# Gate tables of a sparse expert layer: one 256-column product a token instead of a full-precision one, with the row gathers spread over other slots

## The chip, the cores and the metric

One Trainium2 chip, one core. The metric is the device time of one launch in microseconds (us), lower is better. A time is the median of several runs; a profiled execution is one run taken with the hardware profiler.

## The reference

One transformer block in f32 for 256 tokens of width 2048: an input projection, two mixers (a gated linear attention and a compressed, selected and windowed attention), a gated merge, an output projection with residual, and then the part that matters here, a product-key expert layer over 128 x 128 = 16384 experts with 8 heads and 16 picks a head:

```python
v1, i1 = lax.top_k(s1, PEER_TOPK)
v2, i2 = lax.top_k(s2, PEER_TOPK)
cand = (v1[..., :, None] + v2[..., None, :]).reshape(T, PEER_HEADS, PEER_TOPK * PEER_TOPK)
vals, flat = lax.top_k(cand, PEER_TOPK)
e1 = jnp.take_along_axis(i1, flat // PEER_TOPK, axis=-1)
e2 = jnp.take_along_axis(i2, flat % PEER_TOPK, axis=-1)
experts = e1 * PEER_NKEYS + e2
gates = jax.nn.softmax(vals, axis=-1)
...
hid = jax.nn.gelu(jnp.einsum('cd,chkd->chk', xc, u_tab[ec]).astype(jnp.float32))
return jnp.einsum('chk,chkd->cd', (gc * hid).astype(xc.dtype), v_tab[ec])
```

Each token has 128 picks, each a pair (e1, e2) with a gate. The block ends in a norm.

## The kernel before, in words

The kernel doesn't gather the picked experts of most tokens. It streams all 16384 rows of both expert matrices past TensorE in 128 weight units each (1 MB, 128 x 2048) and multiplies the hidden values by a table of gates, 128 x 128 a token, that is zero where nothing was picked. The first 32 tokens (G) are done otherwise: their rows of both matrices are gathered by index, 64 gathers of 128 rows, one row product on VectorE each (`gathered`, L1782). The first half of the gathers are rows of the first matrix.

**Units.** Every weight unit is loaded by SyncE (L339), split into an upper part by ScalarE (`hi_wide`, L577, a copy to the short f32 form) and a lower part by VectorE (`lo_wide`, L1396, weight minus upper part), and used by TensorE in 16 chunks with two products each, 448 and 224 columns (L1265, L1266 in the first pass, L1314, L1315 in the second). Four buffers hold split units; the split of a unit may start when the unit four before it is done (`unit_done`), so ScalarE and VectorE work three units ahead (AHEAD).

**Rounds.** The first pass is 16 rounds i of 8 units k, `hidden(i)` on each engine: TensorE L1249, ScalarE L850, VectorE L1816, GpSimd L503 to L524. After each second unit ScalarE copies the sums out of PSUM (L868), GpSimd adds their two halves (`hidden_sum`, L467), ScalarE applies Gelu (L844) and stores every fourth unit's worth to HBM. In rounds 0 to 7 VectorE also does the routing of 16 groups (`route`, L1721) and GpSimd its lookups (`lookup`, L472). PSUM banks 0 to 3 take the units, banks 4 to 7 are free for tables.

**The table stage** is rounds 8 to 14: two tables of 16 tokens (TB) a round, 14 in all. For each, VectorE writes in `picks_hot` (L1743) a one-hot of e1 for 16 tokens at once (L1754) and, token by token, a one-hot of e2 times the gate (L1758). TensorE multiplies the two for each token, 128 x 128, after units 2 and 6 (`table`, L1285, L1292); both operands are full f32, which the trace shows as two passes a token. ScalarE copies the 16 tables out of PSUM into `gate_a`, rearranged so that the 16 tokens lie side by side (`table_out`, L817, L825), and stores them. `turn_picks` and `picks_out` turn the picks of 128 tokens at a time before that.

**What sets the order** is written by hand: each engine runs its own list in order, with semaphores between them. Row products stand in the slots PRE_SLOTS (L91) of the first pass (32 of them, PRE) and V_SLOTS (L94) of the second (32); GpSimd issues their loads by PRE_ISSUE and one after each hidden_sum from round 8 on. In the second pass VectorE has, in each pair of units, two splits and `weights` (L1806): a product with the gate tables and a subtraction, with a ScalarE copy between.

The lines of VectorE's `hidden` that order the work in a unit:

```python
if k % 4 == 0 and tables:
    tb = i * 2 + (k // 4 - 2 * I_TAB)
...
    picks_hot(tb)
lo_wide(i * 8 + (U0 + k + AHEAD), k + AHEAD)
...
if isinstance(i, int) and (i, k) in pre_slots:
    gathered(pre_slots[i, k])
```

## Time and profile before

| what | us |
|---|---|
| median of 3 runs (2312.88 to 2314.02) | 2313.14 |
| the profiled execution | 2312.33 |
| its span, first to last instruction | 2310.6 |
| TensorE busy in the span | 2277.3 |
| VectorE, ScalarE, GpSimd busy | 1665.7, 1215.1, 472.9 |
| VectorE's 256 lower splits at L1402 | 587.4 |
| ScalarE's 14 table copies at L825 | 54.1 |
| mean granted TensorE clock, as a share of full speed | 0.997 |

The profiled execution is timed as the others are; the rest of it beside the span, 1.7 us, lies before the first and after the last instruction. "Idle before" in a row is the time in which the engine stood still before the instruction, with what released it. A row of a timeline gives start, duration, engine, line, operation and operands. Starts that follow each other more closely than the duration mean that the instructions overlap, as the long rows of products on TensorE and of splits on VectorE do.

### The profile page before, as it was taken

What the parts mean: (1) busy time and instruction counts of PE and PEld (TensorE: products, weight loads), DVE (VectorE), ACT (ScalarE), POOL (GpSimd) and SP (SyncE); (2) the same over time, 40 slices, a digit from 0 to 9 for tenths busy, and PEclk for the clock granted to TensorE, in tenths of its full rate; (3) what the DMA queues carried; (4) which work ended last, traced back from release to release, by engine and by line L of the source; (5) the groups of instructions that cost most, each with busy time, mean ns of one, the idle gap of its engine ahead of it and who ended that gap; (6) DMA issues with size and microseconds to landing.
All of it is one profiled execution on the core that took longest, in us unless ns stands there. A gap on an engine that the chain in (4) does not pass through costs nothing.

```text
span 2310.6 us, 35967 instructions
## 1 busy us (share of the span) xinstructions
PE 2277.3 (99%) x13406; PEld 2074.6 (90%) x13406; DVE 1665.7 (72%) x2049; ACT 1215.1 (53%) x1138; POOL 472.9 (20%) x430
## 2 busy tenths in 40 slices
PE   7999999999999999999999999999999999999997
PEld 6888888888888889999999999999999999999997
DVE  5544776665655555898899989887578778878775
ACT  5534555555454344666666556565544444444443
POOL 0001342100000000243456322222222222122100
PEclk9999999999999999999999999999999999999999
DMA  7756556545456656666676899999999999999982
GB/s 283 271 193 214 209 202 213 196 164 172 169 200 219 223 198 237 224 240 237 227 279 246 318 328 333 331 329 316 353 365 360 362 361 366 364 373 368 355 314 87
DMA packets 122285, 623.73 MB, mean 270 GB/s; under 512 B 12000, under 2 KB 40928, under 8 KB 61776
## 3 DMA queue, kind: packets, MB, share of 16 engines
q1 hardware_dynamic: 58752, 423.65, 49.6%
q0 software_dynamic: 25616, 156.65, 18.2%
q10 hardware_dynamic: 37824, 42.18, 5.1%
q8 instruction: 60, 0.98, 0.2%
q14 instruction: 33, 0.27, 0.0%
HBM read 576.29 MB, written 46.14 MB: 269 GB/s over the span
## 4 chain that ended last, share of the span: by engine, by line
PE 92%; DVE 4%; ACT 2%; DMA 1%; issue 1%; DVEq 0%; POOL 0%; ACTq 0%; SPq 0%; POOLq 0%
PE psum L1314 18%; PE psum L1265 17%; PE psum L957 10%; PE psum L959 10%; PE psum L958 10%; PE psum L1266 9%; PE psum L1315 8%; PE psum L1292 2%; DVE w_lo L1402 1%; PE psum L1091 1%; DMA w_raw<-in_w_units 1%; PE psum L1216 1%; PE psum L1215 1%; PE psum L1217 1%; PE psum L1052 1%
## 5 line engine op out<-in xcount | busy, mean ns | idle before, releaser
L1265 PE MATMUL psum<-h2T,w_hi 128*128 128x448 f32 x2048 | 644.6, 373 | 1.1 <-DVE w_lo L1402 0.7
L1314 PE MATMUL psum<-w_ul,w_hi 128*128 128x448 f32 x2048 | 642.7, 374 | 1.8 <-DVE w_ul L1812 1.8
L1266 PE MATMUL psum<-h2T,w_lo 128*128 128x224 f32 x2048 | 543.3, 265 | 0.0
L1315 PE MATMUL psum<-w_ul,w_lo 128*128 128x224 f32 x2048 | 541.2, 264 | 0.0
L1394 DVE TENSOR_TENSOR w_lo<-w_raw,w_hi 128x2048 fp32r<-128x2048 f32 x144 | 331.3, 2306 | 213.6 <-ACT w_hi L575 213.1
L1314 PEld LDWEIGHTS psum<-w_ul,w_hi 128*128 128x128 f32 x2048 | 384.1, 188 | 31.7 <-issue 2.6
L1265 PEld LDWEIGHTS psum<-h2T,w_hi 128*128 128x128 f32 x2048 | 383.8, 187 | 31.2 <-issue 1.2
L575 ACT ACTIVATE w_hi<-w_raw 128x2048 fp32r<-128x2048 f32 x144 | 275.5, 1913 | 253.3 <-DMA w_raw<-in_w_units 225.2
L1315 PEld LDWEIGHTS psum<-w_ul,w_lo 128*128 128x128 f32 x2048 | 390.7, 191 | 0.0
L1266 PEld LDWEIGHTS psum<-h2T,w_lo 128*128 128x128 f32 x2048 | 390.2, 191 | 0.0
L1402 DVE TENSOR_TENSOR w_lo<-raw_x,w_hi 128x2048 fp32r<-128x2048 f32 x128 | 294.2, 2301 | 76.8 <-ACT w_hi L587 74.7
L1402 DVE TENSOR_TENSOR w_lo<-w_raw,w_hi 128x2048 fp32r<-128x2048 f32 x128 | 293.2, 2292 | 68.2 <-ACT w_hi L587 65.6
L957 PE MATMUL psum<-w_hi,hT_hi 128*128 128x512 f32 x768 | 306.2, 399 | 12.0 <-DVE w_lo L1394 12.0
L959 PE MATMUL psum<-w_hi,hT_lo 128*128 128x512 f32 x768 | 300.5, 391 | 0.0
L958 PE MATMUL psum<-w_lo,hT_hi 128*128 128x512 f32 x768 | 300.1, 391 | 0.0
L587 ACT ACTIVATE w_hi<-w_raw 128x2048 fp32r<-128x2048 f32 x128 | 244.8, 1913 | 99.0 <-PE psum L1315 51.9
L587 ACT ACTIVATE w_hi<-raw_x 128x2048 fp32r<-128x2048 f32 x128 | 244.0, 1908 | 58.0 <-PE psum L1315 37.3
L470 POOL TENSOR_TENSOR hs<-hs 128x448 f32<-128x448 f32 x64 | 105.2, 1643 | 422.9 <-ACT hs L868 416.9
L879 ACT ACTIVATE w_ul<-h_in 128x896 fp32r<-128x896 f32 x64 | 61.0, 954 | 244.3 <-DVE h_in L1809 244.3
L957 PEld LDWEIGHTS psum<-w_hi,hT_hi 128*128 128x128 f32 x768 | 145.0, 189 | 41.2 <-issue 12.9
L959 PEld LDWEIGHTS psum<-w_hi,hT_lo 128*128 128x128 f32 x768 | 144.7, 188 | 31.1
L958 PEld LDWEIGHTS psum<-w_lo,hT_hi 128*128 128x128 f32 x768 | 145.0, 189 | 28.7
(331 smaller groups left out, 2807.3 us busy)
## 6 DMA issues: line engine op xcount, KB each, us to landing
w_raw<-in_w_units SPq DMA_DIRECT2D x272, 1024.0 KB, 5.8
raw_x<-in_w_units SPq DMA_DIRECT2D x128, 1024.0 KB, 6.3
g_tab<-tab_scratch POOLq DMA_DIRECT2D x32, 896.0 KB, 8.0
h_in<-hid_scratch POOLq DMA_DIRECT2D x64, 448.0 KB
hid_scratch<-hst ACTq DMA_DIRECT2D x32, 448.0 KB, 5.1
tab_scratch<-gate_a ACTq DMA_DIRECT2D x14, 1024.0 KB, 7.0
proj_scratch<-evac ACTq DMA_DIRECT2D x24, 512.0 KB, 5.2
x_nat<-in_x POOLq DMA_DIRECT2D x2, 2048.0 KB, 9.2
```

What stands on the lines that cost most here:

```text
L470: pool.tensor_tensor(both, both, hs[:, q, :, NU:2 * NU], ALU.add).then_inc(hid_summed, 1)
L575: act.activation(w_hi[:, s % SPLIT, :], w_raw[:, s % RAW, :], ACT.Copy).then_inc(hi_done, 1)
L587: act.activation(w_hi[:, s % SPLIT, :], src, ACT.Copy).then_inc(hi_done, 1)
L957: pe.matmul(out, xh[:, kc0 + c, ts], rh, start=st, stop=False, skip_group_check=True)
L958: pe.matmul(out, xh[:, kc0 + c, ts], rl, start=False, stop=False, skip_group_check=True)
L959: ins = pe.matmul(out, xl[:, kc0 + c, ts], rh, start=False, stop=en, skip_group_check=True)
L1265: pe.matmul(psum[:, k % 4, 0:2 * NU].rearrange("p (a t) -> p a t", a=2), uh, h2T[:, c, :, G:S], start=c == 0, stop=False, skip_group_check ...
L1266: ins = pe.matmul(psum[:, k % 4, NU:2 * NU], ul, h2T[:, c, 0, G:S], start=False, stop=c == KC - 1, skip_group_check=True)
L1314: pe.matmul(psum[:, c, 0:2 * NU].rearrange("p (a t) -> p a t", a=2), w_hi[:, s, o:o + P], ul, start=first, stop=False, skip_group_check=True)
L1315: return pe.matmul(psum[:, c, 0:NU], w_lo[:, s, o:o + P], ul[:, 0, :], start=False, stop=False, skip_group_check=True)
L1394: dve.tensor_tensor(w_lo[:, s % SPLIT, :], w_raw[:, s % RAW, :], w_hi[:, s % SPLIT, :].bitcast(F32), ALU.subtract).then_inc(lo_done, 1)
L1402: dve.tensor_tensor(w_lo[:, s % SPLIT, :], src, w_hi[:, s % SPLIT, :].bitcast(F32), ALU.subtract).then_inc(lo_done, 1)
```

## The change

Each operand of the table product becomes a short f32 one (F32R): the one-hot of e1 as it is, and the one-hot of e2 times the gate's upper part and times its lower part, side by side in 256 columns. So a token has one product of 256 columns, and the two halves of its result are added afterwards. This is done for 8 tokens (TH) at a time, after units 1, 3, 5 and 7 of rounds 8 to 14, 28 half-tables (NHALF). VectorE writes both one-hots of 8 tokens in one instruction (`picks`), ScalarE scales the second by the upper gate, token by token (`table_slot`), GpSimd by the lower gate (`second_lower`). After the product ScalarE copies the lower results out of PSUM (`lower_out`), ahead of its weight copy in the even units, and VectorE adds them to the upper results, into the rearranged buffer (`table_added`). The store goes out after every second half-table. The rows: 25 in the first pass, 7 of them before round 8 (5 before), 39 in the second pass.

```diff
-PRE = 32
-PRE_EARLY = 5
+TH = TB // 2
+NHALF = 2 * NTAB
+PRE = 25
+PRE_EARLY = 7
...
-PRE_SLOTS = [(5, 3), (5, 7), (6, 3), (6, 7), (7, 3)] + [(I_TAB + (2 * n + 5) // 8, (2 * n + 5) % 8) for n in range(PRE - PRE_EARLY)]
-PRE_ISSUE = {(4, 3): 0, (5, 2): 1, (6, 0): 2, (6, 2): 3, (7, 0): 4}
+PRE_ROUND = {8: (3, 7), 9: (1, 3, 5), 10: (1, 5), 11: (1, 3, 5), 12: (1, 5), 13: (1, 3, 5), 14: (1, 5), 15: (1,)}
+PRE_SLOTS = [(4, 7), (5, 3), (5, 7), (6, 3), (6, 7), (7, 3), (7, 7)] + [(i, k) for i in PRE_ROUND for k in PRE_ROUND[i]]
+PRE_ISSUE = {(4, 2): 0, (5, 0): 1, (5, 2): 2, (6, 0): 3, (6, 2): 4, (7, 0): 5, (7, 2): 6}
...
-V_SLOTS = sorted([(0, 5)] + [(i, k) for i in range(1, U_IT - 1) for k in (1, 5)] + [(2, 7), (6, 7), (10, 7)])
+V_SLOTS = sorted([(0, 5), (0, 7)] + [(i, k) for i in range(1, U_IT - 1) for k in (1, 5)] + [(i, 3) for i in range(2, 11)])
...
+        tables = psum[:, 4:8, :].rearrange("p b (t s c) -> p (b t) s c", s=2, c=PEER_NK)
+        staged = gate_a[:, :, :].rearrange("p a b -> p (a b)").rearrange("p (c t) -> p t c", t=TB)
...
+            def second_lower(hb):
+
+                pool.wait_ge(picks_done, hb + 1)
+                if hb:
+                    pool.wait_ge(tab_done, hb)
+                pool.tensor_tensor(hot2a[:, :, 1, :], picked[:, 1, :, :].bitcast(F32),
+                                   gate_lo[:, G + hb * TH:G + (hb + 1) * TH, None].to_broadcast([P, TH, PEER_NK]), ALU.mult).then_inc(hot2_done, 1)
...
             for i in range(I_TAB, I_END):
                 for j in range(4):
+                    second_lower((i - I_TAB) * 4 + j)
                     hidden_sum(i * 4 + j, j % 2)
...
+            def lower_out(i, k):
+                hb = 4 * (i - I_TAB) + k // 2
+                if 1 <= hb <= NHALF:
+                    act.wait_ge(tab_done, hb)
+                    if hb == 1:
+                        act.wait_ge(lookup_done, ROUTES)
+                    else:
+                        act.wait_ge(tab_out, hb - 1)
+                    act.activation(low[:, :, :], tables[:, :, 1, :], ACT.Copy).then_inc(low_out, 1)
+
+            def table_slot(i, k):
+                hb = 4 * (i - I_TAB) + k // 2
+                if k % 2 == 0:
+                    if hb < NHALF:
+                        act.wait_ge(picks_done, hb + 1)
+                        if hb:
+                            act.wait_ge(tab_done, hb)
+                        for j in range(TH):
+                            t = G + hb * TH + j
+                            ins = act.activation(hot2a[:, j, 0, :], picked[:, 1, j, :].bitcast(F32), ACT.Copy, scale=gate_hi[:, t:t + 1].bitcast(F32))
+                        ins.then_inc(hot2_done, 1)
+                elif k % 4 == 1 and 0 < hb <= NHALF:
+                    tb = hb // 2 - 1
+                    act.wait_ge(tab_out, hb)
+                    act.dma_start(tab[:, :, tb, :].rearrange("g p n -> p g n"),
+                                  gate_a[:, :, :].rearrange("p a b -> p (a b)").rearrange("p (g n) -> p g n", g=U_IT)).then_inc(tab_st, 16)
...
                 for k in range(8):
+                    if tables and k % 2 == 0:
+                        lower_out(i, k)
                     hi_wide(i * 8 + (U0 + k + AHEAD), k + AHEAD)
...
-                    if k % 4 == 3 and tables:
-                        table_out(i * 2 + (k // 4 - 2 * I_TAB))
+                    if tables:
+                        table_slot(i, k)
...
-                    if k % 4 == 2 and tables:
-                        table(i * 2 + (k // 4 - 2 * I_TAB))
+                    if k % 2 == 1 and tables:
+                        table(i * 4 + (k // 2 - 4 * I_TAB))
...
+                pe.wait_ge(picks_done, hb + 1)
+                pe.wait_ge(hot2_done, hb * 2 + 2)
+                if not (isinstance(hb, int) and hb == 0):
+                    pe.wait_ge(tab_out, hb)
+                for j in range(TH):
+                    ins = pe.matmul(tables[:, j, :, :], picked[:, 0, j, :], hot2a[:, j, :, :], start=True, stop=True, skip_group_check=True)
                 ins.then_inc(tab_done, 1)
...
+            def picks(hb):
+
+                if hb:
+                    dve.wait_ge(hot2_done, 2 * hb)
+                    dve.wait_ge(tab_done, hb)
+                dve.tensor_tensor(picked[:, :, :, :], iota[:, None, None, :].to_broadcast([P, 2, TH, PEER_NK]),
+                                  rtT[:, 0:2, G + hb * TH:G + (hb + 1) * TH, None].to_broadcast([P, 2, TH, PEER_NK]), ALU.is_equal).then_inc(picks_done, 1)
+
+            def table_added(hb):
+
+                dve.wait_ge(low_out, hb + 1)
+                if hb == 0:
+                    dve.wait_ge(hg_done, 1)
+                elif hb % 2 == 0:
+                    dve.wait_ge(tab_st, 16 * (hb // 2))
+                dve.tensor_tensor(staged[:, hb % 2 * TH:(hb % 2 + 1) * TH, :], tables[:, :, 0, :], low[:, :, :], ALU.add).then_inc(tab_out, 1)
...
+                    hb = 4 * (i - I_TAB) + k // 2
+                    if k % 2 == 0 and tables and 1 <= hb <= NHALF:
+                        table_added(hb - 1)
+                    if k % 2 == 0 and tables and hb < NHALF:
+                        if G + hb * TH in (G, P):
+                            gates_split((G + hb * TH) // P)
+                        picks(hb)
                     lo_wide(i * 8 + (U0 + k + AHEAD), k + AHEAD)
```

Left out here: buffers and semaphores that are renamed or moved; `gates_split`, which cuts the gates of 128 tokens into their upper and lower parts on VectorE in two small instructions, twice in all; the loads of keys and iota, which now share one semaphore; the gathers' issue rounds on GpSimd (two slots of rows ahead); the row indices, made one unit earlier, in (4, 1); and the Gelu of the gathered rows on ScalarE, which moves from (0, 1) to (2, 7) of the second pass.

## Rows read from the trace of the kernel before

**Rows 1.** The page's first part: busy us (share of the span) x instructions

```profile
PE 2277.3 (99%) x13406; PEld 2074.6 (90%) x13406; DVE 1665.7 (72%) x2049; ACT 1215.1 (53%) x1138; POOL 472.9 (20%) x430
```

**Rows 2.** The chain of waits in the table stage: start us, us, what

```profile
1286.21 5.44 PE psum L1292 x32
1406.52 3.58 PE psum L1292 x32
1430.15 3.58 PE psum L1292 x32
```

**Rows 3.** TensorE's wait (us, times, longest); window: us, PE PEld DVE ACT POOL busy, PEclk, DMA, GB/s

```profile
PE psum L1292 <- DVE hot2a L1758: 1.9, 1, 1.9
1284.00:1292.00 8.00, 6.13 (x38) 5.87 (x37) 7.96 (x14) 2.69 (x3) 2.77 (x1) 0.79 0.36 112
```

**Rows 4.** VectorE in order of time in the table stage: start us, us

```profile
1413.16 2.29 DVE L1754 TENSOR_TENSOR hot1a<-iota,rt 128x2048 f32<-128x2048 f32 x1
1415.37 5.04 DVE L1758 TENSOR_SCALAR hot2a<-iota,rt 128x128 f32<-128x128 f32 x16
```

**Rows 5.** ScalarE's groups by line, mean ns before the last bar

```profile
L825 ACT ACTIVATE gate_a<-psum 128x2048 f32<-128x2048 f32 x14 | 54.1, 3865 | 27.7 <-PE psum L1292 27.7
L587 ACT ACTIVATE w_hi<-raw_x 128x2048 fp32r<-128x2048 f32 x128 | 244.0, 1908 | 58.0 <-PE psum L1315 37.3 <-PE psum L1266 19.3 <-PE psum L1217 1.0
L738 ACT ACTIVATE sm<-sm,nmx 128x128 f32<-128x128 f32 x32 | 12.4, 387 | 0.0
```

**Rows 6.** TensorE in order of time: 256 columns, then the end of a unit

```profile
899.73 0.28 PE L1217 MATMUL psum<-h2T,w_hi 128*128 128x256 f32 x1
899.85 0.28 PE L1215 MATMUL psum<-h2T,w_hi 128*128 128x256 f32 x1
1406.26 0.26 PE L1266 MATMUL psum<-h2T,w_lo 128*128 128x224 f32 x1
1406.36 3.74 PE L1292 MATMUL psum<-hot2a,hot1a 128*128 128x128 f32 x32
```

**Rows 7.** VectorE and GpSimd in order of time in the routing stage

```profile
1252.26 0.69 DVE L1740 TENSOR_TENSOR hot<-abf,iota 128x512 f32<-128x512 f32 x1
1252.87 2.29 DVE L1402 TENSOR_TENSOR w_lo<-raw_x,w_hi 128x2048 fp32r<-128x2048 f32 x1
1253.10 3.21 POOL L474 TENSOR_TENSOR hot<-hot,if_top 128x512 f32<-128x512 f32 x1 [1.20 <-DVE hot L1740]
1255.07 3.38 DVE L1798 CUSTOM_DVE_ANT_0 pre_ring<-pre_ring,g 128x2048 f32<-128x2048 f32 x1
```

**Rows 8.** GpSimd by line: ns min/median/max, first and last start us

```profile
L474 POOL TENSOR_TENSOR hot<-hot,if_top x16: 1284/1301/3350, 970.0 to 1275.2; 128x512 f32<-128x512 f32 x16
L499 POOL TENSOR_TENSOR g<-g,x_rep x1: 4660/4660/4660, 957.7 to 957.7; 128x2048 f32<-128x2048 f32 x1
L470 POOL TENSOR_TENSOR hs<-hs x64: 1147/1294/3302, 962.3 to 1645.3; 128x448 f32<-128x448 f32 x64
```

**Rows 9.** VectorE by line: ns min/median/max

```profile
L1659 DVE TENSOR_TENSOR x_nat<-x_nat,psum x4: 1221/1222/1222, 824.2 to 892.1; 128x1024 f32<-128x1024 f32 x4
L1493 DVE TENSOR_TENSOR blk_c<-kvT_c,posT x4: 1868/1882/1900, 120.9 to 126.2; 128x960 f32<-128x960 f32 x4
```

**Rows 10.** The stores of gate_a: from issue to landing

```profile
DMA to landing us min/median/max: 5.9/7.0/19.5
```

**Rows 11.** VectorE and GpSimd in order of time before the first table

```profile
1277.39 3.15 DVE L1754 TENSOR_TENSOR hot1a<-iota,rt 128x2048 f32<-128x2048 f32 x1
1282.43 0.32 POOL L479 TENSOR_TENSOR rt<-hot 128x32 f32<-128x32 f32 x1
```

**Rows 12.** VectorE in order of time in the routing stage

```profile
1162.45 2.29 DVE L1402 TENSOR_TENSOR w_lo<-w_raw,w_hi 128x2048 fp32r<-128x2048 f32 x1 [1.13 <-ACT w_hi L587]
```

**Rows 13.** Windows of the second expert pass, columns as in group 3

```profile
1725.30:1765.40 40.10, 40.10 (x258) 38.27 (x257) 31.06 (x19) 18.73 (x12) 8.04 (x9) 1.00 0.91 357
1765.40:1805.50 40.10, 40.10 (x258) 38.28 (x257) 33.17 (x20) 18.72 (x12) 10.88 (x10) 1.00 0.96 372
```

More of the change, by code:

```diff
@@ L456, in _ @@
             pool.wait_ge(xt_done, 4)
-            pool.dma_start(keys[:, :, :], io["keys"]).then_inc(keys_in, 16)
-            pool.dma_start(iota[:, :], io["iota"].partition_broadcast(P)).then_inc(iota_in, 16)
+            pool.dma_start(keys[:, :, :], io["keys"]).then_inc(keys_iota_in, 16)
+            pool.dma_start(iota[:, :], io["iota"].partition_broadcast(P)).then_inc(keys_iota_in, 16)
             def v_load(m):
@@ L858, in hidden @@
                         route_exp(i * 2 - 1)
-                    if tile is not None and k == 2 * tile:
+                    if tile is not None and k == tile:
                         picks_out(tile)
-                    if k % 4 == 3 and tables:
-                        table_out(i * 2 + (k // 4 - 2 * I_TAB))
+                    if tables:
+                        table_slot(i, k)
                     if k % 2 == 1:
@@ L886, in _ @@
                 hidden(i, routes=True)
-            hidden(I_TAB, tables=True)
-            hidden(I_PICK1, tile=1, tables=True)
-            with act.Fori(I_PICK1 + 1, I_END) as i:
-                hidden(i, tables=True)
-            hidden(I_END)
+            for i in range(I_TAB, I_END + 1):
+                hidden(i, tile=1 if i == I_PICK1 else None, tables=True)
             hidden_out(U_IT - 1, 3)
@@ L916, in gathered_gelu @@
                 act.activation(hid_g[:, :], dots[:, :], ACT.Gelu_apprx_tanh, scale=rs_g[:, 0:1]).then_inc(hidg_done, 1)
-            experts_out(0, gelu=1)
-            with act.Fori(1, U_IT // 2 - 1) as i:
+            for i in range(2):
+                experts_out(i)
+            experts_out(2, gelu=7)
+            with act.Fori(3, U_IT // 2 - 1) as i:
                 experts_out(i)
@@ L1283, in turn_picks, with table @@
                 ins.then_inc(rt_turned, 1)
-            def table(tb):
-                pe.wait_ge(hot1_done, tb + 1)
-                pe.wait_ge(hot2_done, tb + 1)
-                if not (isinstance(tb, int) and tb == 0):
-                    pe.wait_ge(tab_out, tb)
-                for j in range(TB):
-                    ins = pe.matmul(psum[:, 4 + j // 4, (j % 4) * P:(j % 4 + 1) * P], hot1a[:, j, :], hot2a[:, j, :], start=True, stop=True, skip_group_check=True)
+            def table(hb):
+                pe.wait_ge(picks_done, hb + 1)
[4 more added lines that the diff above has]
+                    ins = pe.matmul(tables[:, j, :, :], picked[:, 0, j, :], hot2a[:, j, :, :], start=True, stop=True, skip_group_check=True)
                 ins.then_inc(tab_done, 1)
@@ L1741, in route, with gates_split @@
                                       iota[:, None, None, 0:TOPK].to_broadcast([P, 2, TOPK, TOPK]), ALU.is_equal).then_inc(lookup_in, 1)
-            def picks_hot(tb, parts=range(5)):
-                hot1, hot2 = hot1a, hot2a
-                for part in parts:
-                    if part == 0:
-                        if not (isinstance(tb, int) and tb == 0):
-                            dve.wait_ge(hot2_done, tb)
-                            dve.wait_ge(tab_done, tb)
-                        dve.tensor_copy(rt16[:, :, :], rtT[:, :, ds(tb * TB + G, TB)]).then_inc(rt16_done, 1)
-                        dve.wait_ge(rt16_done, tb + 1)
-                        dve.tensor_tensor(hot1[:, :, :], iota[:, None, :].to_broadcast([P, TB, PEER_NK]),
-                                          rt16[:, 0, :, None].to_broadcast([P, TB, PEER_NK]), ALU.is_equal).then_inc(hot1_done, 1)
-                    else:
-                        for j in range((part - 1) * TB // 4, part * TB // 4):
-                            ins = dve.tensor_scalar(hot2[:, j, :], iota[:, :], rt16[:, 1, j:j + 1], rt16[:, 2, j:j + 1], ALU.is_equal, ALU.mult)
-                        if part == 4:
-                            ins.then_inc(hot2_done, 1)
+            def gates_split(t):
+                dve.wait_ge(rt_out, t + 1)
+                cols = slice(t * P, (t + 1) * P)
+                step(dve.tensor_copy(gate_hi[:, cols], rtT[:, 2, cols]))
+                dve.tensor_tensor(gate_lo[:, cols], rtT[:, 2, cols], gate_hi[:, cols].bitcast(F32), ALU.subtract)
+            def picks(hb):
[11 more added lines that the diff above has]
+                dve.tensor_tensor(staged[:, hb % 2 * TH:(hb % 2 + 1) * TH, :], tables[:, :, 0, :], low[:, :, :], ALU.add).then_inc(tab_out, 1)
             def gather_rows():
@@ L1833, in hidden @@
                         clear_pads()
-                    if isinstance(i, int) and (i, k) in pre_slots:
+                    if (i, k) in pre_slots:
                         gathered(pre_slots[i, k])
@@ L1847, in _ @@
                 hidden(i, routes=True)
-            for i in range(I_TAB, I_END):
+            for i in range(I_TAB, I_END + 1):
                 hidden(i, tables=True)
-            hidden(I_END)
             def experts_out(i, last=False):
```

73 lines of the change are left out of this document (31 added, 42 removed).

## The prediction, made before the changed kernel ran

> **What bounds the kernel now.** The page first: TensorE is busy 2277.3 of 2310.6 us [rows 1]. Then the chain of waits through the table stage (the last 7 of 16 rounds of the first expert pass): it runs on TensorE's products and its tables, and a table of 16 tokens starts each 23.63 us, 3.58 of it the table, the rest four weight units, so 5.01 a unit [rows 2]. TensorE waits there for nothing but, once, the first table [rows 3]. So TensorE time saved is time saved, as long as the other engines' chain from one table to the next stays under TensorE's.
>
> **What is removed.** 13 tables at 3.58 = 46.5 us. The first cost more: its waiting of 1.9 us, then 5.44, with the granted clock at 0.79 in the 8 us around it, that is partly at the lower of the two levels (1.2 GHz) after TensorE had idled [rows 2, 3]; together 7.3. Sum 53.8. VectorE loses the first one-hot and the 16 scaled ones of every 16 tokens (2.3 + 5.0) [rows 4], ScalarE its 3.86 us copy [rows 5]. Fourteen of these go.
>
> **What is added on TensorE.** 28 half-tables of 8 products, each 256 columns. Such products start 0.12 us apart in the query stage [rows 6]: 0.96, with the restart 1.04, and 29.1 in all. Bounds: nothing less than 0.10 (the 224-column product's step [rows 6]), at most the 0.22 that a token takes now, 3.58 for 16. With every new wait hidden that is 53.8 - 29.1 = 24.7 us gained.
>
> **The chain that replaces it.** The buffer of one-hots is single, PSUM is single (8 tokens x 256 columns fill banks 4 to 7), so table h+1 can't be prepared beside table h: product, ScalarE's copy of the lower half, VectorE's table_added, VectorE's picks, then ScalarE's 8 scaled copies and GpSimd's second_lower side by side, then the next product. Count from x, the end of one picks on VectorE:
> - VectorE's weight split is queued directly behind: to x+2.2 (start to start 2.21 [rows 4]).
> - GpSimd gets its signal at x but both read two SBUF operands. In the routing stage the same sequence stands: VectorE's one-hot ends at 1252.95, its split starts, GpSimd's multiply, released by that one-hot, takes 3.21 instead of 1.30, ending 1.15 after the split, and the row product behind, with as many elements as the split's 2.29, takes 3.38 [rows 7, 8]. They exclude each other, and the one that waits gets the next turn. The Trainium skill agrees (GPSIMD Engine Reference, "Key points": the SBUF interfaces are shared, with contention where VectorE has two SBUF inputs).
> - second_lower has 1024 elements: between half of 4.66 and 1.30 plus its share of the rest, 2.3 to 2.4 [rows 8]. It runs from x+2.2 to x+4.6; there the next table may start.
> - ScalarE: 8 scaled copies of 128. The nearest row takes 0.39 each, with overlap and accumulation [rows 5]; on the slope from its larger copies 0.2. I take 0.24: 1.9, then its weight copy 1.8: x+3.8. VectorE's second split waits for the multiply: x+4.6 to x+6.8.
> - GpSimd's hidden_sum (1.1 at its shortest [rows 8]) has its turn next, to x+7.9; if this round has a row, 2.2 more, to x+10.1.
> - table_added: a. picks: 2.2. The next x is at x + 12.3 + a.
>
> **The value of a.** It adds 1024 elements from PSUM and SBUF and writes them 64 bytes apart. Lower end 1.22, the same shape written densely [rows 9]. But ScalarE's present copy writes this very pattern and takes 3.86 for 2048, where a dense one takes 1.91 [rows 5], and VectorE reading 960 elements 64 bytes apart takes 1.88 [rows 9]. Both are 1.8 to 1.9 ns an element, so a = 2.0, the nearest rows in layout. Two pages of the Trainium skill differ here: VectorE: DVE Perf Modes ("Mode 1×") says of that mode that weird strides and PSUM operands "all work" at one result a cycle, which would give the lower end; SBUF — State Buffer ("Door 1: The DMA port swizzle", the note on cachelines) says that each access in a new 16-byte line pays a penalty. The trace's reads bear out the second; no run here shows the write on VectorE.
>
> **Rounds.** A round with a row therefore takes 14.3 us. One without: TensorE sets it, 10.02 + 1.04 = 11.06, since the chain (0.96 product, 1.1 copy, 2.0, 2.2, 4.6 = 10.9) just fits. In rounds of even number a second wait enters: VectorE's next table_added overwrites what ScalarE stores, and the store is issued after the second weight copy, at x+3.8, and lands 5.9 to 7.0 later [rows 10]: next x = x+3.8+5.9+2.0+2.2 = 13.9 to 15.0. With fewer rows on the queues I take the lower part, level with 14.3. Of 27 rounds 17 have a row between (the slots of round 8 to (14,5)), one even round has none: 18 x 14.3 + 9 x 11.1 = 357.3.
>
> **The first table.** Due after 2 units instead of 3. VectorE reached its one-hots at 1277.4, 8 us late; the row added at (7,7) moves that by 3.1, splitting the gates by 0.6, so picks end near 1283.5, the last lookup on GpSimd ends at 1282.75 [rows 11], and second_lower at about 1288: TensorE waits 8.9 us.
>
> **The sum over the stage.** Before: 12 units (60.2) + 7.3 + 13 x 23.63 = 374.6. After: 10 units (50.1) + 8.9 + 357.3 + 1.0 = 417.4. That is +42.8. Behind the new waits stand, on ScalarE, the weight copies (three units ahead of need), and on GpSimd hidden_sum and the row loads, each ahead of its user by a round: nothing beyond the turns counted. SyncE's weight loads wait for the second splits and follow TensorE at its new pace: nothing. picks_out, the Gelu of the rows, and the wait for keys and iota together move into idle time: nothing; if they did not, under 1 us each. Before the stage, one row more at (4,7): VectorE idles only 1.13 us for ScalarE afterwards [rows 12] and is behind at the end, so of 2.3 to 3.4 us some 2.0 reach TensorE (0 to 3.4). In the second pass 7 rows more: a stretch with a third row has VectorE at 33.2 of 40.1 us instead of 31.1, DMA at 0.96 instead of 0.91, TensorE full in both [rows 13]; 0.5 (0 to 3). Sum +45.3 on the profiled execution's 2312.33, which is 0.8 under the median of the runs: 2358.
>
> **The rivals.** *Cheap add* (a = 1.22): a row round's chain is 13.5, of which an isolated one hides 0.9 in the slack of the round before: about 13.1, 18 x 1.2 less: 2336. For: the dense rows; against: both strided rows. The rule of the Trainium skill's VectorE: DVE Perf Modes ("Mode 1×") is this case. *Stores late or clock low*: landing at 7.0 or more adds 0.8 in 13 even rounds, and waits of 3 us may let the clock fall as at the first table, each such table then 1 us longer where it is on the chain (9): 2368. For: the median landing, the 0.79. *The cover holds* (the other side): GpSimd's multiply and sum run beside VectorE's splits and rows. Then 3.5 us of the row round's chain are gone; the point at which it decides is 11.06, which needs a near 1.2 and landing near 5.9 as well. Stage: 50.1 + 8.9 + 27 x 11.06 + 1.0 = 358.6, -16.0, with 2.5 of rows elsewhere 2299; with the remaining row slips up to 2308. Against: [rows 7]. For: stores and lookups move where the traffic is thinner, and records of GpSimd are rough. That the products are slower than 0.12 would sit inside the waits of the slow rounds; at the upper bound the nine fast ones grow by 0.8, 7 us.
>
> **How the numbers follow.** Chances: forecast 0.38, cheap add 0.24, late stores or clock 0.15, cover holds 0.18, something between that ends level 0.05. Range 2302 to 2374: from inside the case in which the cover holds to the late case with some microseconds more; outside stay most of the first and the tail of the last. A measurement of this kernel tells about 0.2% (4.6 us) from no change. Faster 0.18, same 0.05, slower 0.77.
>
> **What would show it.** Right: TensorE waits for GpSimd's second_lower before most tables, some 3 us where a row lies between, none or little where none does; second_lower near 4.3 us against 2.4 of work; VectorE's strided add near 2.0; store to landing 6 to 7 with VectorE waiting for it in some even rounds; the first table near 9 us late. Wrong: no waits for second_lower and tables 11.06 apart (cover holds), table_added at 1.2, or TensorE waits in the second pass.

## The result, and the profile after

The changed kernel takes 2354.7 us (median of 4 runs, 2352.55 to 2357.04), the kernel before 2313.0 beside it: a ratio of 1.0182, 95% interval 1.0169 to 1.0194. It is 1.8% slower; 2358 was forecast. The profiled execution took 2352.55, its span is 2350.9, 40.3 more than before.

The first part of its page answers to [rows 1]:

```profile
PE 2273.0 (97%) x13182; PEld 2063.6 (88%) x13182; DVE 1689.0 (72%) x1857; ACT 1249.4 (53%) x1376; POOL 624.8 (27%) x458
```

TensorE is busy 4 us less in a span 40 longer, and GpSimd has 152 us more. By the starts of the weight units on TensorE the 40.3 split up so: the part from the first unit to unit (8,0) takes 327.6 instead of 325.4 (+2.2), the table stage, from (8,0) to the first unit of the second pass, 411.6 instead of 376.0 (+35.6), the second pass to the end 668.7 instead of 666.6 (+2.2); the start of the first unit differs by 0.2.

What TensorE waits for in the table stage (us, times, longest), where [rows 3] had 1.9 us once:

```profile
PE psum L1332 <- POOL hot2a L503: 32.9, 12, 9.0
PE psum L1332 <- issue: 7.0, 4, 2.6
```

L1332 are the table's products, L503 is second_lower. The longest wait, 9.0, is the first table. From there the tables start 11.1 to 15.4 apart, where the kernel before kept its 23.63 for two halves [rows 2]. Here is one round with a row, in order of time, first VectorE, then ScalarE and GpSimd (start us, us):

```profile
1451.52 2.27 DVE L1795 TENSOR_TENSOR picked<-iota,rtT 128x2048 fp32r<-128x2048 f32 x1
1453.71 2.27 DVE L1442 TENSOR_TENSOR w_lo<-w_raw,w_hi 128x2048 fp32r<-128x2048 f32 x1
1458.12 2.29 DVE L1442 TENSOR_TENSOR w_lo<-raw_x,w_hi 128x2048 fp32r<-128x2048 f32 x1 [2.14 <-ACT w_hi L613]
1460.33 3.25 DVE L1842 CUSTOM_DVE_ANT_0 pre_ring<-pre_ring,g 128x2048 f32<-128x2048 f32 x1
...
1463.51 1.94 DVE L1805 TENSOR_TENSOR gate_a<-psum,low 128x1024 f32<-128x1024 f32 x1
1465.30 2.27 DVE L1795 TENSOR_TENSOR picked<-iota,rtT 128x2048 fp32r<-128x2048 f32 x1
...
1453.83 2.46 ACT L862 ACTIVATE hot2a<-picked,gate_hi 128x128 fp32r<-128x128 f32 x8 [2.54 <-DVE picked L1795]
1456.19 1.90 ACT L613 ACTIVATE w_hi<-raw_x 128x2048 fp32r<-128x2048 f32 x1
...
1453.87 3.87 POOL L503 TENSOR_TENSOR hot2a<-picked,gate_lo 128x1024 fp32r<-128x1024 f32 x1 [3.10 <-DVE picked L1795]
1459.03 2.40 POOL L487 TENSOR_TENSOR hs<-hs 128x448 f32<-128x448 f32 x1 [1.29 <-ACT hs L909]
```

Read it from x, the end of the picks, at 1453.79. VectorE splits to x+2.2, then waits 2.14 us; its second split starts at x+4.33, the row at 6.54, the add at 9.72, the next picks at 11.5, and the next x is 13.78 later. Ten of the 17 rounds with a row take this long (13.70 to 13.78), six take longer and wait for the store, and one takes 12.86. VectorE's wait is for ScalarE's weight copy (ends at x+4.30), which stands behind the eight scaled copies (2.46 together). second_lower ends at x+3.95, with 3.87 for a work that took 1.89 the one time that VectorE left it alone (the first), and the row takes 3.25 instead of 2.28 because hidden_sum has a turn in it. TensorE's product can start at x+4.0, so TensorE waits for GpSimd, but the loop that sets the pace runs through VectorE's own list and its 2.14 us wait for ScalarE's weight copy.

VectorE's own waits in the stage, the ones for w_lo before the first table included (us, times, longest):

```profile
DVE w_lo L1442 <- ACT w_hi L613: 74.7, 36, 6.0
DVE gate_a L1805 <- DMA tab_scratch<-gate_a: 8.1, 6, 2.1
DVE gate_a L1805 <- ACT low L851: 4.1, 5, 1.9
```

27 rounds take 351.4 from the first x to the last: 17 with a row between, 233.9 at 13.76 and 5.9 more, mostly the store's; and 10 without, 111.6 (10.65 where nothing disturbs). The granted clock falls in eight stretches of the stage, one beside the 9.0 us wait and seven beside waits of TensorE of 1.9 to 4.2 us; one wait of 2.5 us, at 1589.5, is left without. Two windows, columns as in [rows 3]:

```profile
1420.00:1430.00 10.00, 9.25 (x60) 8.57 (x58) 8.56 (x6) 3.83 (x6) 2.26 (x2) 1.00 0.64 253
1430.00:1440.00 10.00, 7.03 (x31) 6.70 (x32) 7.14 (x6) 7.34 (x10) 6.27 (x3) 0.66 0.61 212
```

0.66 over 10 us is some 7 at 1.2 GHz and the rest at 2.4. TensorE had waited 3.7 us for the table at 1432.97; its eight products then took 2.08 instead of the usual 1.21. In the windows of 10 us from 1280 to 1660 this adds up to 44 us at the lower level. It costs little, since most of it eats waiting that would be there anyway: what it delays on the loop is the lower copy, and VectorE waited for that 4.1 us in all, whatever the clock's part in it.

### The profile page after: what moved, and what is told of

It reads as the page before. It is cut to its first block, busy times and chain, and to the rows that moved or that the text cites. A ratio compares the mean times of both kernels' runs of the same rounds, so it can differ in the third digit from the quotient of the medians.

```text
span 2350.9 us, 35582 instructions
## 1 busy us (share of the span) xinstructions
PE 2273.0 (97%) x13182; PEld 2063.6 (88%) x13182; DVE 1689.0 (72%) x1857; ACT 1249.4 (53%) x1376; POOL 624.8 (27%) x458
## 4 chain that ended last, share of the span: by engine, by line
PE 77%; DVE 10%; ACT 5%; issue 4%; DMA 3%; POOL 1%; ACTq 0%; DVEq 0%; SPq 0%; POOLq 0%
PE psum L1354 17%; PE psum L997 10%; PE psum L999 10%; PE psum L1305 10%; PE psum L998 10%; PE psum L1355 8%; PE psum L1306 5%; DVE w_lo L1442 3%; DVE picked L1795 3%; ACT w_hi L613 2%; DMA tab_scratch<-gate_a 2%; ACT hot2a L862 2%; PE psum L1131 1%; POOL hot2a L503 1%; DVE gate_a L1805 1%
## 5 line engine op out<-in xcount | busy, mean ns | idle before, releaser
L1305 PE MATMUL psum<-h2T,w_hi 128*128 128x448 f32 x2048 | 656.3, 378 | 2.0 <-DVE w_lo L1442 2.0
L1305 PEld LDWEIGHTS psum<-h2T,w_hi 128*128 128x128 f32 x2048 | 390.5, 191 | 33.7 <-issue 3.0
L1306 PEld LDWEIGHTS psum<-h2T,w_lo 128*128 128x128 f32 x2048 | 396.6, 194 | 0.0
L997 PE MATMUL psum<-w_hi,hT_hi 128*128 128x512 f32 x768 | 305.9, 398 | 13.3 <-DVE w_lo L1434 13.3
L997 PEld LDWEIGHTS psum<-w_hi,hT_hi 128*128 128x128 f32 x768 | 144.7, 188 | 42.8 <-issue 14.6
L487 POOL TENSOR_TENSOR hs<-hs 128x448 f32<-128x448 f32 x64 | 123.1, 1923 | 219.3 <-ACT hs L909 193.9
```

Source lines behind the costliest of these rows:

```text
L487: pool.tensor_tensor(both, both, hs[:, q, :, NU:2 * NU], ALU.add).then_inc(hid_summed, 1)
L997: pe.matmul(out, xh[:, kc0 + c, ts], rh, start=st, stop=False, skip_group_check=True)
L1305: pe.matmul(psum[:, k % 4, 0:2 * NU].rearrange("p (a t) -> p a t", a=2), uh, h2T[:, c, :, G:S], start=c == 0, stop=False, skip_group_check ...
L1306: ins = pe.matmul(psum[:, k % 4, NU:2 * NU], ul, h2T[:, c, 0, G:S], start=False, stop=c == KC - 1, skip_group_check=True)
```

## The experiments

**Which of two links holds the second split.** The forecast's step was GpSimd's turn, the trace says ScalarE's copy. Three kernels, one edit each and both together; the first edit leaves out seven eighths of the lower multiply:

```diff
-                pool.tensor_tensor(hot2a[:, :, 1, :], picked[:, 1, :, :].bitcast(F32),
-                                   gate_lo[..., None].to_broadcast([P, TH, PEER_NK]), ALU.mult).then_inc(hot2_done, 1)
+                n = 1 if hb else TH
+                pool.tensor_tensor(hot2a[:, 0:n, 1, :], picked[:, 1, 0:n, :].bitcast(F32),
+                                   gate_lo[..., None].to_broadcast([P, n, PEER_NK]), ALU.mult).then_inc(hot2_done, 1)
```

> From the changed kernel (2354.7 us); GpSimd's second_lower multiplies the full 8 tokens for the first half-table only, and 1 token of 8 from then on (the lower part of the gates of the other 7 is left out of the tables). Forecast's step (GpSimd's turn on the operand interfaces is what the second weight split waits for): the second split starts at x+2.2 to x+3.9 instead of behind the multiply, and each row round loses about 2: 17 x 2 = 34 us, 2321. Rival A, from the trace of after: the second split starts 4.33 after the picks end because ScalarE's weight copy, queued behind the eight scaled copies, ends at 4.29, and the multiply ends at 3.95; then the split stays at 4.33, row rounds stay at 13.76, only the product comes some 1.5 us sooner and waits on ScalarE's copies: within 4 us of the changed kernel, 2351 to 2356.

```diff
-                    hi_wide(i * 8 + (U0 + k + AHEAD), k + AHEAD)
+                    if not (tables and k % 2 == 1):
+                        hi_wide(i * 8 + (U0 + k + AHEAD), k + AHEAD)
+                    if tables and k % 2 == 0:
+                        hi_wide(i * 8 + (U0 + k + 1 + AHEAD), k + 1 + AHEAD)
```

> From the changed kernel; ScalarE makes the weight copy of the odd unit ahead of the eight scaled copies instead of behind them. Nothing is left out. ScalarE idles up to 6.5 us before the picks, so the copy is finished by x and costs the scaled copies nothing. Rival A of the first run: the second split no longer waits for ScalarE, but then GpSimd's multiply, which has its turn from 2.2 to 3.95, is what it waits for: it starts at 3.95 instead of 4.33, so a row round takes 13.4: 17 x 0.38 = 6.5 us less, 2348. If ScalarE alone held it (no exclusion), the split would start at 2.2 and a row round would take 11.7: 2318. Forecast's step: 4.6 for the multiply's end stays, so no gain: 2354.

> Both edits together: 1 token of 8 in GpSimd's multiply, and the odd unit's weight copy ahead of the scaled copies. If the two links (ScalarE's copy, GpSimd's turn) stand side by side, each hiding the other, then only both together pay: the second split starts at 2.2 to 2.5, a row round takes 13.76 - 2.1 = 11.7, the others are set by TensorE at 11.06: 17 x 2.1 = 36 us less, 2319, and the waits of TensorE nearly go. If the sum of the two single runs is all (6.5 us), some third thing (the row, the store, the copy of the lower half) sets the round.

Measured, in that order: 2353.7 (2348.1 to 2356.4), 2349.2 (2343.9 to 2355.3) and 2333.8 (2331.4 to 2336.5). In the first, a row round still takes 13.77, and TensorE waits no less than before, now for ScalarE's scaled copies (31.7 us, 12 times, beside 9.1 for the first table): taking GpSimd's work away alone gave nothing. (Even with one token of 8 its record is 2.38 long, since it waits for its turn behind the first split.) The second split in the three kernels, in that order, from the rows in order of time (start us, us), with GpSimd's multiply behind it in the second:

```profile
1458.97 2.29 DVE L1443 TENSOR_TENSOR w_lo<-raw_x,w_hi 128x2048 fp32r<-128x2048 f32 x1 [2.13 <-ACT w_hi L614]
```

```profile
1453.74 4.00 DVE L1445 TENSOR_TENSOR w_lo<-raw_x,w_hi 128x2048 fp32r<-128x2048 f32 x1
...
1451.71 3.87 POOL L503 TENSOR_TENSOR hot2a<-picked,gate_lo 128x1024 fp32r<-128x1024 f32 x1 [6.24 <-DVE picked L1798]
```

```profile
1463.64 2.50 DVE L1446 TENSOR_TENSOR w_lo<-w_raw,w_hi 128x2048 fp32r<-128x2048 f32 x1
```

With the copy first, the split is issued at once but takes 4.00: it stands still while GpSimd's multiply has its turn after the first split, and ends 0.5 earlier than in the changed kernel. A row round takes 13.27; in the medians the 5 us are within the spread of the runs. With both links gone it takes 2.50 and most row rounds come to 10.9 to 11.6. So the two links stand side by side, each hiding the other, as expected for the third run. But it came out 15 us above the 2319 expected, most of it in the next wait:

```profile
DVE gate_a L1809 <- DMA tab_scratch<-gate_a: 31.0, 5, 8.8
```

Five rounds of this kernel, of 15.4 to 21.2 us, are those in which the add waits for the store. The faster loop uncovers it.

**The row and the store.** The rows' VectorE work cut to a sixteenth, and the store cut to a sixteenth (both leave the rest of that work out):

```diff
+                if PRE_EARLY <= n < PRE:
+                    row = row[:, 0:128]
+                    ins = dve.tensor_tensor_reduce(row, row, hg[:, 0:128], 1.0, 0.0, ALU.mult, ALU.add, dots[:, j:j + 1])
+                    ins.then_inc(ring_used, 1)
```

> From the changed kernel; the 18 rows numbered 7 to 24 are still loaded, but VectorE multiplies 128 of their 2048 elements (the dot products of these rows are left out). It prices the row in the round. Forecast: a row costs 14.3 - 11.1 = 3.2 in each of 17 rounds, 54 us of the stage, 2300. From the trace of after: VectorE's row of 3.24 goes, the chain of a round is 10.6 and TensorE sets 11.06, so 17 x 2.7 = 46 us less, less what the store's landing keeps in even rounds (up to 5 us): 2309 to 2314. Rival: the store of the even rounds sets the pace without the rows too (13.9 in 13 rounds): 2335 or more.

```diff
-                    act.dma_start(tab[:, :, tb, :].rearrange("g p n -> p g n"), gate_a[...]).then_inc(tab_st, 16)
+                    act.dma_start(tab[0:1, :, tb, :].rearrange("g p n -> p g n"), gate_a[...][:, 0:1, :]).then_inc(tab_st, 16)
...
-                pool.dma_start(g_tabs[i % 2][:, :, :], tab[i % U_IT]).then_inc(vt_in[i % 2], 16)
+                pool.dma_start(g_tabs[i % 2][:, :, :], tab[0]).then_inc(vt_in[i % 2], 16)
```

> From the changed kernel: each store of a finished table writes group 0 of its 16 groups only, and the second pass reads group 0 each time (so 15 of 16 parts of each table are left out, the transfers of the second pass stay in size). It prices the wait for the store and its traffic. The trace of after shows 8.1 us of VectorE's waiting for it in 6 even rounds; in row rounds all of it is on the path: 8 us less, 2346.5, the even rounds all at 13.76. Forecast's step (store issued at x+3.8, landing 5.9 to 7.0, even rounds 13.9 to 15.0, level with the row's 14.3) gives at most 1 to 2 us: 2353. Rival: thinner traffic also speeds the row loads and weight loads: nothing waits for these, so no more than 8.

Short rows: 2342.4 (2334.0 to 2344.5), 12 us less where 41 to 46 had been expected. Two things took the place of the row. Its short form still takes 1.25 where hidden_sum has its turn, so such a round takes 11.8, not 10.6; and the add waited 24.9 us for stores instead of 8.1. The row in order of time, and VectorE's wait:

```profile
1470.57 1.25 DVE L1843 CUSTOM_DVE_ANT_0 pre_ring<-pre_ring,g 128x128 f32<-128x128 f32 x1
```

```profile
DVE gate_a L1805 <- DMA tab_scratch<-gate_a: 24.9, 6, 5.9
```

Short store: 2346.2 (2343.1 to 2347.3), the 8 us as expected, and 13 of the 17 row rounds at 13.76 or 13.77, the other four shorter. The store is worth 8 us as the kernel stands, and more as soon as the loop gets shorter.

**The add.** Its elements walked in the other order, and written densely (which leaves out their placing in the table):

```diff
-                dve.tensor_tensor(staged[...], tables[:, :, 0, :], low[:, :, :], ALU.add).then_inc(tab_out, 1)
+                dve.tensor_tensor(staged[...].rearrange("p t c -> p c t"), tables[:, :, 0, :].rearrange("p t c -> p c t"),
+                                  low[:, :, :].rearrange("p t c -> p c t"), ALU.add).then_inc(tab_out, 1)
```

> From the changed kernel, nothing left out: table_added walks its 1024 elements column by column with the 8 tokens innermost (reads of PSUM and low far apart, writes in runs of 32 bytes) instead of token by token (reads dense, writes 64 bytes apart, 1.95 us). If the spacing of the writes alone makes the 1.95 (the forecast's reason for a = 2.0), it falls to near the dense 1.22 and 17 row rounds give 12 us: 2342. If spacing on the reading side costs as much (one operand or two), it stays at 1.9 or rises to 2.5 or more, and the round with it: 2354 to 2370.

```diff
-                dve.tensor_tensor(staged[:, hb % 2 * TH:(hb % 2 + 1) * TH, :], tables[:, :, 0, :], low[:, :, :], ALU.add).then_inc(tab_out, 1)
+                dve.tensor_tensor(gate_a[:, hb % 2 * TH:(hb % 2 + 1) * TH, :], tables[:, :, 0, :], low[:, :, :], ALU.add).then_inc(tab_out, 1)
```

> From the changed kernel; table_added writes its half-table densely instead of 64 bytes apart (the placing of the entries in the table is left out, the store sends the same bytes). It prices the spacing of the writes. If the spacing is what takes 1.95, the add falls to about 1.22 (the dense row of the kernel before) and 17 row rounds give 0.73 each: 12 us, 2342. If it is the read from PSUM or the pairing of PSUM with SBUF, it stays near 1.95 and nothing changes: 2354.

The add by line (ns min/median/max), in the changed kernel, in the other order, and dense:

```profile
L1805 DVE TENSOR_TENSOR gate_a<-psum,low x28: 1871/1952/2010, 1294.1 to 1643.5; 128x1024 f32<-128x1024 f32 x28
```

```profile
L1805 DVE TENSOR_TENSOR gate_a<-psum,low x28: 1981/2013/2076, 1295.2 to 1643.2; 128x1024 f32<-128x1024 f32 x28
```

```profile
L1805 DVE TENSOR_TENSOR gate_a<-psum,low x28: 1212/1219/1226, 1294.2 to 1645.4; 128x1024 f32<-128x1024 f32 x28
```

The write's spacing is the whole difference: dense it is 1.22, the lower bound of the forecast. The other order, with dense runs of 32 bytes on the writing side and the spacing on the reading side, is no better (2354.8, 2353.7 to 2362.8). And yet the dense add made no faster kernel: a row round without another wait takes 13.13, as it should, but the median is 2363.2 (2354.4 to 2373.9). What the slower runs lost, no trace shows; in the profiled one, the fastest at 2354.4, the store's waits took back what the add gave:

```profile
DVE gate_a L1805 <- DMA tab_scratch<-gate_a: 27.5, 8, 4.8
```

Its stores took 10.3 us to land (median) against 7.4. What goes with a late landing is in the traces of the transfers. In the changed kernel seven of the 14 stores land in 5.5 to 6.1 us, and while each is under way 0.3 to 0.4 MB of weight units are moved; the other seven land in 8.7 to 11.5 us, with 1.3 to 2.2 MB. In the dense kernel the four latest, 13.4 to 14.1 us, have 2.3 to 2.4 MB and a whole row load of 1 MB beside them. The DMA engines are near full either way: over the 5.6 us store issued at 1467.72 they move 275 GB/s, over the 10.2 us one at 1492.13 354. So the late store shares them with other loads, and a loop of another length sets it against others; the last version below shows it by moving the rows.

**The rows' new places alone**, put into the kernel before:

> From the kernel before: only its row slots are set as in the changed kernel (7 rows before the table stage instead of 5, 18 in it instead of 27, 39 in the second pass instead of 32, with the Gelu of the rows moved accordingly); tables as before. Forecast's terms: +2.0 before the stage, +0.5 in the second pass, nothing in the stage: 2315.8. From the trace of after, second pass +2.3 and before the stage +2.5: 2317.5. Rival: fewer rows in the stage let VectorE and the queues breathe and give back about as much: 2313.

```diff
-PRE = 32
-PRE_EARLY = 5
+PRE = 25
+PRE_EARLY = 7
...
-V_SLOTS = sorted([(0, 5)] + [(i, k) for i in range(1, U_IT - 1) for k in (1, 5)] + [(2, 7), (6, 7), (10, 7)])
+V_SLOTS = sorted([(0, 5), (0, 7)] + [(i, k) for i in range(1, U_IT - 1) for k in (1, 5)] + [(i, 3) for i in range(2, 11)])
```

Measured 2322.2, a ratio of 1.0043 (1.0027 to 1.0059): 9 us for an edit that I had priced at 2.5. TensorE's waits for the first table and in the second pass:

```profile
PE psum L1304 <- DVE hot2a L1770: 4.1, 1, 4.1
...
PE psum L1326 <- DVE w_ul L1824: 2.7, 4, 1.8
```

The first unit started 1.0 later here, as it differs by up to 2.7 between profiled runs anyway. The part up to (8,0) cost 3.9 more, the round of the first table 2.5, since VectorE comes to it later, and the middle of the second pass 2.1: the round in which VectorE sums the first half of the output takes 43.7 instead of 41.6, most likely because round 7 now has a third row ahead of it (no run tries that alone). In the changed kernel the part before the stage costs 2.2 and the middle of the second pass 2.2. Why the same two rows before the stage cost 3.9 here and 2.2 there, no run separates; the first table is late there by its own chain.

**A version with all of it.** First, on top of the copy first (2349.2), the lower multiply moved to VectorE:

```diff
+                dve.wait_ge(picks_done, hb + 1)
+                dve.tensor_tensor(hot2a[:, :, 1, :], picked[:, 1, :, :].bitcast(F32), gate_lo[...], ALU.mult).then_inc(hot2_done, 1)
```

> From the run with the weight copy first (2349.2 us), all work done: the lower multiply goes from GpSimd to VectorE, directly behind the picks. There its 1024 elements should take 1.2 instead of GpSimd's 1.85 of turn, and the product is ready at x+2.5 instead of 3.95. If operand turns are what fills a round (picks 2.1, splits 4.4, row 2.3, add 1.95 on VectorE, and 1.75 + 1.0 of GpSimd in between, sum 13.3), a row round takes 13.3 - 1.75 + 1.25 = 12.8, and 17 of them give 9 us: 2340. If GpSimd's turns cost VectorE nothing beyond its own busy time, VectorE's work grows by 1.25 a round instead: 27 x 1.25 = up to 34 us more, 2370 or above. TensorE should wait for ScalarE's scaled copies or nothing instead of GpSimd.

2348.8 (2336.5 to 2350.6). There it takes 1225 ns, a row round 12.86 where the copy first alone had 13.27, as summed, and TensorE's product may start at x+2.7, when the scaled copies end. But the add waited 32.5 us for stores. So the operand turns are what fills a round, and it is the store again that hides the gain. Then a second staging buffer in the place of the second row buffer and 14 rows in every second round, with this and the copy first, and without:

```diff
-        region(AT_MIX, AT_MIX + 16 * KB, ("pre_ring", [P, 2, D]))
+        region(AT_MIX, AT_MIX + 16 * KB, ("pre_ring", [P, 1, D]), ("gate_b", [P, TB, PEER_NK]))
...
-PRE_ROUND = {8: (3, 7), 9: (1, 3, 5), 10: (1, 5), 11: (1, 3, 5), 12: (1, 5), 13: (1, 3, 5), 14: (1, 5), 15: (1,)}
+PRE_ROUND = {8: (5,), 9: (1, 5), 10: (1, 5), 11: (1, 5), 12: (1, 5), 13: (1, 5), 14: (1, 5), 15: (1,)}
```

> All work done; the version that the runs so far suggest. From the run with the lower multiply on VectorE (2348.8 us, VectorE waiting 32.5 us for stores): a second staging buffer of 8 KB in place of the second row buffer, so that a store has two tables' time; 14 rows in the stage in place of 18, one in every second round; 43 in the second pass in place of 39. A row round's chain is then 12.85 and one without 9.7, 22.55 a pair against 22.1 on TensorE: 27 rounds at 11.2 to 11.3. Stage: 50.1 + 9 + 27 x 11.25 + 1 = 364 against 411.6 of the changed kernel; 4 more rows in the second pass 0 to 2. So 2306 (2303 to 2312), below both kernels. Rival: the row buffer, single now, makes VectorE wait for row loads of 7 us and more: then 14 rounds get some microseconds each, 2320 or above.

> From the changed kernel, all work done: only the second staging buffer and the 14 rows in every second round (43 in the second pass), with ScalarE's order and GpSimd's multiply left as the change has them. A row round 13.76, one without 10.65, 24.4 a pair against 22.1 on TensorE, no store waits: 13.5 x 24.4 = 329.6 in place of 351.0 for the 27 rounds: 2354.7 - 21.4 + 1 = 2334. If it comes out near the version with all levers instead (2306), the rows and the store were the whole loss and the chain of operand turns did not matter.

2313.0 (ratio 0.9999, 0.9990 to 1.0008) with all, 2337.7 with the buffer and the rows alone: 17 of the 42 us lost come back from these two, 25 more from the two edits of the operand turns. In neither does the add wait for a store. With all edits the stage took 362.5 (364 expected), 13.4 less than in the kernel before, and TensorE hardly waits in it; but the second pass took 9.2 more and the part before the stage 2.6, which gave it back. TensorE's waits from the stage into the second pass, and the VectorE instruction that makes the fourth block of weights:

```profile
PE psum L1332 <- ACT hot2a L859: 9.8, 9, 7.3
PE psum L1354 <- DVE w_ul L1859: 5.1, 2, 4.2
```

```profile
1666.24 1.09 DVE L1856 TENSOR_TENSOR h_in<-h_in,g_tab 128x896 f32<-128x896 f32 x1 [6.50 <-DMA h_in<-hid_scratch]
```

Its first round takes 47.25 instead of 41.14 (45.61 with the buffer and the rows alone). One more kernel makes two edits at once: the first row loads of the second pass are issued later, and the rows of the stage stand one round earlier each:

```diff
-            for n in range(PRE, PRE + RING):
-                gather(n)
...
+                if m == 2:
+                    for n in range(PRE, PRE + RING):
+                        gather(n)
...
+PRE_ROUND = {i: (3, 7) for i in range(8, 15)}
```

> From the version with all levers (2313.0 us; its stage came out at 362.5 as worked out, but its second pass took 7.9 us longer from its first unit to the middle than the changed kernel's: the load of the fourth block of hidden values, issued 13.3 us after the pass begins into queues that three row loads had filled from 3.9 us on, took near 19 us to land, and TensorE waited up to 4.2 at a time). Two edits, all work done: the first three row loads of the second pass are issued behind that load instead of ahead of it (their rows are used 38 us into the pass), and the rows of the table stage go one round earlier each, so that the last one ends before the last table is stored. If the row loads in front are the cause, the first round of the second pass is back at 41.2 and the second at 40.1: 7 us less, 2306, 0.3% faster than before. If the cause is something else in the shorter stage (the last stores of table and hidden values landing late), it stays within 2 us of 2313.

2309.8 (2308.7 to 2310.8), ratio 0.9986, interval 0.9977 to 0.9995: with 3 us the only version that is faster than the kernel before, and by less than the 0.2% named as what a measurement tells. The first round of the second pass is back at 41.14, the second takes 41.66. That the row loads ahead of the hidden values were the cause isn't shown by it: the two edits aren't separated, and the changed kernel issues the same three row loads in front, 3.7 to 6.3 us into the pass, and has 41.14 too. The stage took 366.8, 4.3 more than with the rows in the other rounds, which I had not expected: there the first rounds of the stage kept to 22.0 a pair, here 22.5 from the start, with hidden_sum's turn in the row, and VectorE waited 2.8 us for row loads.

The two kernels show more of the store, since in the stage they differ by the places of the rows alone. With the rows one round earlier all 14 stores land in 5.1 to 5.8 us: no row load is under way beside them, and the next weight unit is issued 3.6 us behind 13 of them (up to 0.3 MB moves meanwhile). In the version before, 12 of 14 land in 12.8 to 14.9 us, each beside a row load and 2.1 to 2.8 MB of weight units. So the places of the rows alone move the landing from 5 us to 13.

## Why the prediction was right

The sign and the mechanism held, a loop of VectorE's work and GpSimd's turns that is longer than TensorE's: 2358 forecast, 2354.7 measured, from a stage of +42.8 (measured +35.6), and 2.0 and 0.5 elsewhere (2.2 and 2.2). The stage of the kernel before is 376.0 in its trace and was added up as 374.6, that of the changed kernel 411.6 and not 417.4. That the end comes so close is chance in part: the sum was 5 us too long for the profiled execution, and the median of the changed kernel's runs lies 2.2 above its profiled one, where 0.8 had been added. By its own steps:

- **TensorE's side.** The eight products take 0.96, starts 0.12 apart, where the clock is full. Of the 27 tables behind the first, TensorE waits before 15, 0.95 to 4.2 us each; the forecast had some 3 us where a row lies between. The first table was forecast to wait 8.9 and waited 9.0; there the picks ended 2.0 later than forecast and second_lower 1.8, but TensorE came 1.8 later too.
- **second_lower.** The exclusion of [rows 7] is there: 3.87 beside a split, 1.89 without. Its work was mis-sized, 2.4 for 1.89, so it ends at x+3.95, not 4.6. The Trainium skill (SBUF — State Buffer, "Terms", shared port pair) calls it an exclusive lock held for a whole instruction, where the loser fully blocks; the 4.00 us split beside the 3.87 multiply agrees.
- **The scaled copies.** This was the step that named the wrong releaser. They were put at 1.9 together and took 2.46 (0.39 each, starts 0.29 apart), so that the weight copy ends at 4.30 and not 3.8 and is what the second split waits for. With the multiply's turn mis-sized as well, the two errors nearly cancel: x+4.33 against the 4.6 forecast, which is luck. The first run showed that GpSimd alone is not the link, the third that both are.
- **hidden_sum's turn and the row.** Forecast to x+10.1, measured 9.72: 1.0 of turn, 2.2 of row.
- **a.** 2.0 forecast, 1.95 measured, and 1.22 dense. Of the two pages weighed, the Trainium skill's VectorE: DVE Perf Modes ("Mode 1×"), read as one result a cycle at any spacing, would give 1.22 here and is not borne out; the cacheline note of its SBUF — State Buffer ("Door 1: The DMA port swizzle") points the right way.
- **A row round** comes to 13.76 against 14.3, 9 us less for 17 of them, and the even round without a row, taken at 14.3 for its store, had no such wait and took 11.24, 3 less. The store's waits on top of the row gave 6 of these 12 us back, so the rounds were forecast 6 us too long. Rounds without a row: 11.1 forecast, 11.16 measured on average (10 of them; 10.6 to 10.7 in the five in which the add and the splits have no other wait than VectorE's usual one).
- **The stores.** Here the picture was off and the size not: issued at x+3.8 and landing after 5.9 to 7.0, they were forecast to hold each even round level with the row. They are mostly issued at x+0.15 and land after 5.5 to 11.5 us, and the add waited in 6 of 13 rounds, 8.1 us, which the short store gave back (8.5 by the medians).
- **The rows elsewhere.** 2.0 before the stage was near the 2.2 of the changed kernel, though the same rows cost 3.9 in the kernel before. The 0.5 for the second pass was 2.2, all of it in the round in which the first half of the output is summed (43.7 instead of 41.6), a place that the windows of [rows 13] don't show.

Of the rivals, Cheap add had its price right (13.1 a row round, 13.13 measured with the dense add), not its condition, and the kernel that met the condition took 2363 and not 2336. Stores late or clock low was half there: landings of up to 11.5 us with 8.1 of waiting, the clock low for 44 us with at most 4.1 on the loop. The cover holds was excluded by the 3.87.

## What to carry to other kernels

Before splitting one step in two so as to halve a buffer, add up what one turn of the loop costs the engine that runs it: here VectorE's five instructions and the turns GpSimd takes between them come to 13.3 us (13.27 measured with the copy first) against the 11.06 that TensorE left, and no wait need be named for that. Where a trace names a releaser, look at who comes second: two links 0.35 us apart hid each other; removing the one gave nothing and the other 0.5 a row round, both 2.9. And a transfer that lands late inside a slow loop is a wait in a fast one: four separate edits each shortened the round and lost part or all of it to the same store, until the rows' loads stood elsewhere or the store had a second buffer.

## What the runs showed of the hardware that was not expected

ScalarE issued the store ahead of copies that stand before it in the program. In the changed kernel, ScalarE in order of time (ACTq is its queue's issue):

```profile
1467.60 0.40 ACT L862 ACTIVATE hot2a<-picked,gate_hi 128x128 fp32r<-128x128 f32 x1 [5.54 <-DVE picked L1795]
1467.72 0.38 ACTq L867 DMA_DIRECT2D tab_scratch<-gate_a  x1
1467.91 2.14 ACT L862 ACTIVATE hot2a<-picked,gate_hi 128x128 fp32r<-128x128 f32 x7
1469.96 1.89 ACT L613 ACTIVATE w_hi<-w_raw 128x2048 fp32r<-128x2048 f32 x1
```

By the program the store comes behind all eight copies and the weight copy; it is recorded 0.12 after the first of them, and so 3.7 us earlier than the forecast had it. Its wait, for the add, had been met 2 us before. The record isn't a slip: the store's packets of 512 bytes run from 1468.61 to 1472.86, so they start before the weight copy does.

The exclusion between VectorE and GpSimd works in both directions. The multiply of 1.89 us took 3.87 behind a split. A row of 128 elements took 1.25 us on VectorE beside hidden_sum, and a split 4.00 beside second_lower, each time because GpSimd's instruction was already waiting when VectorE's turn ended; the next turn then is GpSimd's, even if VectorE has its following instruction at hand. Moving the multiply to VectorE, which looks like loading the busier engine, shortened the row round by 0.4, since its 1.23 there replaces 1.75 of GpSimd's turn.

The same 1 MB store in pieces of 512 bytes lands in 5.1 us or in 14.9, with nothing about the store itself changed: what counts is how much of row loads and weight units is moved beside it.
